# Two-block fp32 network on one core: norm rows transposed and scaled in one TensorE product with a diagonal matrix

## The reference, cut to what matters

```python
def rmsnorm(x, gain):
    xf = x.astype(jnp.float32)
    y = xf * lax.rsqrt(jnp.mean(xf * xf, axis=-1, keepdims=True) + EPS)
    return (y * gain.astype(jnp.float32)).astype(x.dtype)

h = rmsnorm(x, mix_pre_gain[layer]);  proj = h @ w_in[layer]        # norm 0
h = rmsnorm(x, mlp_pre_gain[layer]);  u = relu(h @ w_up[layer])     # norm 1
h = rms_norm(x, norm_g[l]) * (1.0 + scale) + shift;  z = h @ w_in[l]  # norms 2 and 3 (l = 0, 1)
```

## Time and profile before

| | |
|---|---|
| median of 3 runs | 1962.86 us (1962.75 to 1962.90) |
| the profiled execution, its own time | 1962.09 us |
| its span | 1960.3 us |
| PE busy | 1937.5 us, 99% |
| PEld busy | 1676.0 us, 85% |
| DVE busy | 1527.2 us, 78% |
| ACT busy | 1069.3 us, 55% |
| instructions on DVE, ACT | 2100, 1549 |

### The profile page before, as it was taken

How to read it: one execution, slowest core, us unless ns; L and a number is a source line. 1 busy time by engine, 2 the same in 40 slices (tenths; PEclk the granted TensorE clock), 3 DMA queues, 4 the chain that set the end, 5 groups by cost and what they waited for, 6 DMA issues and landing times.

```text
span 1960.3 us, 27681 instructions
## 1 busy us (share of the span) xinstructions
PE 1937.5 (99%) x11418; PEld 1676.0 (85%) x11418; DVE 1527.2 (78%) x2100; ACT 1069.3 (55%) x1549; POOL 0.2 (0%) x4
## 2 busy tenths in 40 slices
PE   7999999999999999999999999999999999999999
PEld 6888888888888888888888889899888898998887
DVE  6587776868887777888877567999966669999764
ACT  5474766465664433555543475554764566456742
POOL 0000000000000000000000000000000000000000
PEclk9999999999999999999999999999999999999999
DMA  7443445948899998999988634544455455454453
GB/s 284 153 163 123 142 151 197 359 136 299 326 343 335 330 332 324 334 332 337 333 335 335 249 125 167 189 166 139 162 188 181 147 192 174 151 172 136 171 194 122
DMA packets 63982, 442.58 MB, mean 226 GB/s; under 512 B 7249, under 2 KB 7537, under 8 KB 12401
## 3 DMA queue, kind: packets, MB, share of 16 engines
q1 hardware_dynamic: 61920, 434.30, 61.8%
q10 hardware_dynamic: 1936, 6.51, 0.9%
HBM read 438.67 MB, written 2.11 MB: 225 GB/s over the span
## 4 chain that ended last, share of the span: by engine, by line
PE 95%; DVE 3%; ACT 1%; DMA 0%; issue 0%; ACTq 0%; DVEq 0%
PE PS L630 23%; PE PS L632 12%; PE PS L509 11%; PE PS L511 11%; PE PS L510 11%; PE PS L578 6%; PE PS L501 6%; PE PS L579 6%; PE PS L580 6%; DVE WL L1085 1%; PE PS L657 1%; DMA X<-in_x 0%; ACT WH L1930 0%; DVE Y L1127 0%; ACT S L1993 0%
## 5 line engine op out<-in xcount | busy, mean ns | idle before, releaser
L1930 ACT ACTIVATE WH<-RAW 128x1024 fp32r<-128x1024 f32 (+1 forms) x636 | 663.4, 1049 | 742.1 <-PE PS L511 276.4
L1085 DVE TENSOR_TENSOR WL<-RAW,WH 128x1024 fp32r<-128x1024 f32 (+1 forms) x636 | 766.3, 1209 | 370.3 <-ACT WH L1930 369.3
L630 PE MATMUL PS<-HT,WH 128*128 128x512 f32 x2040 | 723.3, 398 | 0.1
L632 PE MATMUL PS<-HT,WL 128*128 128x256 f32 x2040 | 571.6, 280 | 0.0
L630 PEld LDWEIGHTS PS<-HT,WH 128*128 128x128 f32 x2040 | 382.5, 188 | 94.1 <-issue 7.2
L632 PEld LDWEIGHTS PS<-HT,WL 128*128 128x128 f32 x2040 | 385.5, 189 | 0.1
L578 PE MATMUL PS<-HT,WH 128*128 128x256 f32 x880 | 254.6, 289 | 1.0 <-DVE HT L1136 0.7
L580 PE MATMUL PS<-HT,WL 128*128 128x256 f32 x880 | 249.3, 283 | 0.0
L579 PE MATMUL PS<-HT,WH 128*128 128x256 f32 x880 | 249.3, 283 | 0.0
L1094 DVE SCALAR_TENSOR_TENSOR RAW<-RAW,CB 128x2048 f32<-128x2048 f32 x96 | 219.4, 2285 | 0.0
L511 PE MATMUL PS<-WH,Ul 128*128 128x512 f32 x512 | 203.0, 396 | 0.0
(11 more groups left out here) (319 smaller groups left out, 2029.9 us busy)
## 6 DMA issues: line engine op xcount, KB each, us to landing
RAW<-in_w_in SPq DMA_DIRECT2D x112, 1024.0 KB, 4.9
RAW<-in_ada_w SPq DMA_DIRECT2D x96, 1024.0 KB, 6.8
RAW<-in_w_up SPq DMA_DIRECT2D x64, 1024.0 KB, 6.7
RAW<-in_w_down SPq DMA_DIRECT2D x64, 1024.0 KB, 6.2
RAW<-in_w_out SPq DMA_DIRECT2D x48, 1024.0 KB, 4.9
RAW<-in_w_pw SPq DMA_DIRECT2D x8, 1024.0 KB, 4.8
RAW<-in_w_in SPq DMA_DIRECT2D x8, 768.0 KB, 4.3
RAW<-in_w_q_up SPq DMA_DIRECT2D x6, 1024.0 KB, 5.2
```

What stands on the lines that cost most here:

```text
L630: e.matmul(bk[i][:, 0:512], wh[:, at], m["HT"][:, kt, :, :].rearrange("p a t -> p (a t)"), start=kt == 0, stop=False, skip_group_check=True)
L632: op = e.matmul(bk[i][:, 0:256], wl[:, at], HTh[:, kt, :], start=False, stop=kt == n.kts - 1, skip_group_check=True)
L1085: e.tensor_tensor(m[f"WL{j % NHL}"][:, 0:nk * w], m[f"RAW{i % NRAW}"][:, k0 * w:(k0 + nk) * w], m[f"WH{j % NHL}"][:, 0:nk * w].bitcast(F32 ...
L1930: e.activation(m[f"WH{j % NHL}"][:, 0:nk * w], m[f"RAW{i % NRAW}"][:, k0 * w:(k0 + nk) * w], ACT.Copy).then_inc(signals["high"], 1)
```

## The change

`scaled(t)` no longer scales X. It scales the 128 x 128 identity by the 128 factors of token tile t and writes that diagonal matrix to the first 128 columns of Y[:, t]. `turn` on PE multiplies: the X tile is the stationary operand, the diagonal the moving one, so the product is X transposed, each column (token) scaled. It is an ordinary fp32 matmul instead of a transpose. In a step all products with token tile 0 come first, and the banks of the whole step are waited for at its start. The eight calls of `scaled` for a norm become two; the four between the steps of a turn are gone, and their waits with them. ACT's and DVE's parts of `turn`, `keep_warm` and the order of the weights are as before.

```diff
-TURNED_BY = ((2, 4, 6, 8), (3, 4, 6, 8), (3, 4, 6, 8), (3, 4, 6, 8))
     def turn(q):
-        for kt in range(16):
-            b = small()
-            pe.wait_ge("id", 16)
-            pe.wait_ge("xs", 8 * q + TURNED_BY[q][kt // 4])
+        step = 4 if q == 1 else 2
+        for first in range(0, 16, step):
+            banks = [small() for _ in range(step)]
             for tt in range(2):
-                op = e.transpose(bank[b][:, 128 * tt:128 * tt + 128], Y[:, tt, 128 * kt:128 * kt + 128], ident)
-            op.then_inc(signals["turned"], 1)
-            free[b] = ("ht_l", 16 * q + kt + 1) if q < 2 else ("ht_v", 16 * (q - 2) + kt + 1)
-            if kt % (4 if q == 1 else 2) == (3 if q == 1 else 1):
-                yield
+                pe.wait_ge("xs", 2 * q + tt + 1)
+                for kt, b in enumerate(banks, first):
+                    op = mm(b, 128 * tt, 128 * tt + 128, X[:, tt, 128 * kt:128 * kt + 128], Y[:, tt, 0:128], True, True)
+                    if tt:
+                        op.then_inc(signals["turned"], 1)
+            for kt, b in enumerate(banks, first):
+                free[b] = ("ht_l", 16 * q + kt + 1) if q < 2 else ("ht_v", 16 * (q - 2) + kt + 1)
+            yield
...
-    def scaled(t, *cs):
-        for c in cs:
-            e.tensor_scalar(Y[:, t, 512 * c:512 * c + 512], X[:, t, 512 * c:512 * c + 512], ST[:, 54 + t:55 + t], None,
-                            ALU.mult).then_inc(signals["xs"], 1)
+    def scaled(t):
+
+        dve.wait_ge("id", 16)
+        e.tensor_scalar(Y[:, t, 0:128], ident, ST[:, 54 + t:55 + t], None, ALU.mult).then_inc(signals["xs"], 1)
...
-    for c in range(2):
-        scaled(0, c)
-        scaled(1, c)
+    scaled(0)
+    scaled(1)
     course.start(turn(0))
     course.cut_ahead(1)
     course.beat()
-    for c in range(2, 4):
-        scaled(0, c)
-        scaled(1, c)
     course.cut_ahead()
...
     course.start(turn(1))
     course.beat()
-    scaled(0, 2)
-    scaled(1, 2)
     course.cut_ahead(1)
     course.beat()
-    scaled(0, 3)
-    scaled(1, 3)
     course.cut_ahead()
```

More of the change, by code:

```diff
@@ L483, in tensor_program @@
     free = {}
-    HTh, HTl, Y, VT = m["HTh"], m["HTl"], m["Y"], m["VT"]
+    HTh, HTl, X, Y, VT = m["HTh"], m["HTl"], m["X"], m["Y"], m["VT"]
     def split(*_):
@@ L1656, in rows_normed @@
         row_rstd(54)
-        scaled(0, 0, 1)
+        scaled(0)
         row_sum(55, 1, 48, 4, "x_sq", 8 * r + 12)
         row_rstd(55)
-        scaled(1, 0, 1)
+        scaled(1)
     UR = [flat(VT[:, 2 * i:2 * i + 2, :]) for i in range(2)]
```

## The result

The changed kernel takes **1970.88 us** (median of 6 runs, 1969.76 to 1973.43), the kernel before, run beside it, 1962.88 us (6 runs, 1962.75 to 1963.26). The ratio is 1.0042, 95% interval 1.0032 to 1.0052: slower by 8.0 us, where 9.7 were predicted. The profiled execution took 1969.76 us; its span is 1968.0 us, 7.7 more than before.

What follows compares the result with a forecast made beforehand. PE, busy for 1937.5 of 1960.3 us, was taken as the bound. The turns' +2.6, +1.3, +3.1 and +2.7 us make +9.7, so 1972.6 us against the median of 1962.86; range 1968.5 to 1977.

Steps and rivals of the forecast that it cites:

- The bound, and the sign: PE is full, so delays out of a turn stay; slower by more than 3.9 us was given 0.92.
- The price of a product: PE's steps: records set the price; four products 0.90 us instead of 0.36, extra 0.54; eight 1.70 instead of 0.79.
- rival 4: In PE's steps a product costs four transposes, 1.44 us for a step of four; 1994.7 us, chance 0.03.
- Rival 1: Not slower: the second record of a product is free, only gains of 4.3 us left; 1958.6 us, chance 0.03.
- rival 2: Most of the cost hidden by an earlier clock, DVE relief and products at 0.21; 1966.5 us, chance 0.05.
- rival 3: Nothing hidden: the wait for all banks stalls PE as long as the scaling did; 1979.5 us, chance 0.07.
- Turn 0: First three steps cost nothing (−0.1), the five left cost 0.54 each; sum +2.6 us.
- the step on the clock: In turn 0 the clock rises at about 17 us as before; its range −0.4 to +1 us.
- Turn 1: Head −0.2, three steps of eight 2.7, part back as DVE's scalings go; sum +1.3 us, between +0.7 and +2.5.
- Turn 2: Head +0.2, next step +0.54 less 0.33 for DVE's scaling, then five at 0.54; sum +3.1 us.
- Turn 3: As turn 2, but the idle 0.90 before it makes the head −0.2; sum +2.7 us.
- DVE: Over four norms DVE is spared about 12 us, nearly all worth nothing; PE starts at about 11.6 us.

Runs made afterwards that it cites:

- b1: The kernel before with each transpose replaced by an fp32 product of the same Y tile with the identity, all scalings kept on DVE; 1972.19 us, ratio 1.0054.
- a1: The changed kernel run again with nothing edited; 1970.07 us, ratio 1.0041.
- c1: The changed kernel with its products turned back into transposes of X, the norm's row factor left out of the result; 1960.65 us, ratio 0.9992.
- h1: The changed kernel with each product of 128 moving columns done as two of 64; 1999.1 us, ratio 1.019.
- e1: The changed kernel with each PSUM bank waited for right before its first product, not all at the head of a step; 1969.74 us, ratio 1.0038.
- k1: The kernel before with transposes ordered by token tile within a step, each bank waited for one by one; 1962.89 us, ratio 1.0005.
- k2: k1 with the scalings of the later chunks moved from DVE to GpSimd; 1961.14 us, ratio 0.9995.
- g1: The kernel before with 30 fp32 products of a zeroed tile as PE's first work; 1961.99 us, ratio 1.0002.
- k3: k2 with 30 fp32 products of a zeroed tile as PE's first work; 1960.65 us, ratio 0.9993.
- k4: k3 with the transposes back in the order of the kernel before; 1960.42 us, ratio 0.9991.
- g3: e1 with 30 fp32 products of a zeroed tile as PE's first work; 1968.46 us, ratio 1.0033.

## Why the prediction was right, and where it missed

**The bound, and the sign.** Right. What is added to a full PE stays: from the dummies of turn 2 on, the delay of the changed kernel is the same at both ends of each stretch between turns (2.64 after 2.63, 5.43 and 5.43). The one exception is right behind turn 0, where 0.33 us came back; b1 and a1 show 0.34 and 0.35. PE's timeline has it in one place, the first weight product on the last step's tiles, before and after:

```profile
29.13 0.28 PE L580 MATMUL PS<-HT,WL 128*128 128x256 f32 x1
29.52 0.36 PE L578 MATMUL PS<-HT,WH 128*128 128x256 f32 x1
```

```profile
30.41 0.28 PE L579 MATMUL PS<-HT,WL 128*128 128x256 f32 x1
30.53 0.28 PE L577 MATMUL PS<-HT,WH 128*128 128x256 f32 x1
```

Before, PE paused there (0.39 us from start to start instead of 0.12); c1 has the same pause, and there the view names DVE's low part as the releaser. The prediction had no such pause in its account. b1, with all scalings kept, loses the pause as well, so it is the slower steps that give DVE the time.

**The price of a product.** The basis was right, records and not columns (h1), and so was the ratio's size: 0.81 to 0.36 is 2.25. The step of four was mis-sized: 0.90 from rows of other products, 0.81 measured, below both ends of 0.85 to 0.92. The extra is 0.45 instead of 0.54; over the 17 steps this is 1.5 us, the largest part of the miss (+9.7 predicted, +7.7 by the spans, +8.0 by the medians). The factor of 4 that the Trainium skill gives the transpose mode for FP32 (TensorE: Matmul & The Clock Gate, Terms) would make a step 1.44; each one took 0.81, a ratio of 2.25, and the measurement decides: rival 4 is out. Rival 1 is out by the same number, rivals 2 and 3 by the totals, though two parts of rival 2 came true, the earlier clock and the price near 0.21.

**Turn 0.** +2.6 predicted, +1.28 and +1.78 in two executions. Five steps at 0.81 take off 0.45. The rest is the step on the clock: I had it rise at 17 us as before; it rose at 15.0 in the first execution and at 16.1 in the second. The weight product expected at 18.3 started at 17.39 and 17.88. This moment is chance, and half a microsecond of agreement or miss goes with it. The bound of −0.4 for the clock was too narrow.

**Turn 1.** +1.3 predicted, +1.68 measured. The head is as worked out (the first weight product 0.14 us less behind the dummies than before, 0.2 predicted). The steps of eight are 1.70 to 1.78, where 1.70 was taken. What I had too low is the wait for all banks, "ready when the low part of the fourth tile is out": e1 prices it at 0.75 us, and without it the turn costs +0.94. The reason that I gave for what comes back was wrong. From the first dummy to the first weight product, and from one step's first weight product to the next one's, in us (differences to before in brackets):

```
        head          step 2        step 3        step 4
before  7.88          2.30          2.99          4.63
b1      8.59 (+0.71)  3.22 (+0.92)  3.22 (+0.23)  4.56 (-0.07)
after   7.74 (-0.14)  3.47 (+1.17)  3.71 (+0.72)  4.56 (-0.07)
e1      7.75 (-0.13)  3.20 (+0.90)  3.22 (+0.23)  4.57 (-0.06)
```

Three steps at 0.91 would be 2.73; they cost 1.08 in b1 and 1.07 in e1. So 1.7 us come back whether the four scalings stand in DVE's queue (b1) or not (e1): before, PE paused within steps 3 and 4 (1.37 us each from start to start instead of 0.79), and the slower products fill these pauses. DVE's relief pays at the head alone, 0.85 us between b1 and after. That +1.3 came near +1.68 is in part luck: too little was taken as filled, and too little as waited for the banks.

**Turn 2.** +3.1 predicted, +2.79 measured: 0.36 at the head (0.2 predicted), 0.12 for the next step, and five times 0.46. Six steps at 0.81 instead of 0.90 make 0.5 us, more than the miss of 0.3; the head took 0.16 of it back. The next step's 0.12 is not due to the missing scalings either: b1, which has them, shows the same 0.12.

**Turn 3.** +2.7 predicted, +2.28 measured: −0.15 at the head (−0.2 predicted), the rest steps of 0.81. Of the wait of 0.90 before it, which was to be gone, 0.24 is left.

**DVE.** A diagonal takes 0.29 us by itself, and two in a row 0.48, so the second adds the 0.19 that I drew from two wider rows; PE starts at 11.68 (11.6 predicted). The view of lines has line 1127 busy for 13.9 us before and line 1129 for 2.2 after, 11.7 less, near the 12 predicted. DVE's busy time as a whole fell by only 8.8, since it counts overlapping instructions once. PE's rose by 11.8, within the 10 to 14. Of all this the total got back 2.1 us (c1, and b1 against after), nearly all of it at the starts of turns 0, 1 and 3.

## What to carry to other kernels

When one engine makes up the chain, price a trade in its records alone, and take what it saves elsewhere only at the waits that end on the relieved engine: here 256 records of 0.10 us were added for 128 of 0.09, and the 11.7 us spared on DVE brought back 2.1. Where the engine already pauses inside a stretch, slower instructions of its own cost less than their price, whatever the other engine is spared: run the slower instructions alone (b1) before crediting the relief. Take the price of a step from start to start in the timeline; that of the nearest other products was 10% off. An idle engine can carry slow work for a busy one where the consumer's pace allows it; here that took 1.75 us off k1, with a small charge on DVE's own instructions, though k2 stands only 0.8 us below the kernel before, within its interval.

## What was unexpected of the hardware

- A PE made fast early can fall back if it then waits: behind idle times of 0.72 and 2.06 us the granted clock was 0.50 (g1), while with 0.70 and 0.65 us (k3) the records stayed fast. The length of one idle time doesn't decide it: k4 fell behind 1.91 us, and g3 did not behind 2.02, nor g1 behind its first of 2.71. What does isn't shown.
- At the very start the windows give a granted clock of 1.00 although the records follow at 0.21 us, the pitch that g1 shows at 0.50. That 1.00 is no reading: the trace's record of the clock begins only at 17.2 us (before), 15.0 (after) and 16.1 (a1), where the pitch becomes fast. Up to there the pitch is to be trusted. The start of the fast pitch wandered by about 1 us, and with it the run-to-run spread.
- fp32 records of 64 columns hold PE as long as those of 128 (0.106 and 0.101 us).
- Weight products ran 2% slower for almost 60 us behind turn 1 in the four kernels that transpose by token tile (k1, k2, k3, c1), with PE busy throughout; the cause is open.
- Beside a busy GpSimd, some of DVE's instructions took longer (1.56 us instead of 1.21 for one of 1024 columns, k2 and k1).
